# A two-block model on one core: the order of a linear layer's products, its waits, and its fillers

## The reference

```
first block:  proj = rmsnorm(x) @ w_in            (1024 x 3080), forgetting attention and chunked attention
              x += rmsnorm(y @ w_out)
              memory attention: h @ w_mq, mem @ w_mk, mem @ w_mv, o @ w_mo ; x += rmsnorm(...)
              x += rmsnorm(square(relu(h @ w_ff1)) @ w_ff2)
second block: mod = silu(c) @ ada_w + ada_b        (2 x 1024 x 6144)
              layer 0: gated 31-tap convolution (conv_in, depthwise conv, layer norm, silu, conv_out)
              layer 1: hgrn2 mixer (hgrn_in, a scan over time in both directions, hgrn_out)
              each followed by x += g2 * (square(relu(h @ w1)) @ w2)
out = rmsnorm(x)
```

## Time and profile before

| | |
|---|---|
| median of 3 runs | 2157.0 us |
| the profiled execution | 2156.95 us, its span 2155.2 us |
| TensorE (PE) busy | 2095.5 us, 97%, 10728 matmuls |
| VectorE (DVE) busy | 1237.6 us, 57% |
| ScalarE (ACT) busy | 826.2 us, 38% |
| GpSimd (POOL) busy | 202.1 us, 9% |
| mean granted TensorE clock | 0.995 of full speed |
| the chain that ended last | PE 84%, DVE 6%, ACT 5%, DMA 3% |
| linear layers' high products, line 1292 | 1672 and 768, 397 and 390 ns |

### The profile page before, as it was taken

The page is one execution under the profiler, slowest core; times in us unless marked ns, Lnnn a source line. Parts: engine busy times, 40 slices in busy tenths (PEclk is TensorE's granted clock), DMA queues, the critical chain, the costliest instruction groups (busy, mean ns, idle before and its releaser), DMA issues.

```text
span 2155.2 us, 26708 instructions
## 1 busy us (share of the span) xinstructions
PE 2095.5 (97%) x10728; PEld 1649.1 (77%) x10728; DVE 1237.6 (57%) x1895; ACT 826.2 (38%) x1326; POOL 202.1 (9%) x174
## 2 busy tenths in 40 slices
PE   8999999999999999999999999999999999999998
PEld 7777887678878876665788888787777777888886
DVE  5665745445677777887544344365675755443443
ACT  5345544445323233225423223344464454232231
POOL 1321011011000004453000000100000010000001
PEclk9999999999999999999999999999999999999999
DMA  6322422015677762662242332221121232323331
GB/s 202 98 66 90 137 97 92 25 59 206 223 270 249 259 230 87 164 168 82 81 133 97 97 99 89 62 69 50 59 69 50 69 105 83 106 98 98 98 98 40
DMA packets 218555, 245.51 MB, mean 114 GB/s; under 512 B 9144, under 2 KB 203192, under 8 KB 212288
## 3 DMA queue, kind: packets, MB, share of 16 engines
q1 hardware_dynamic: 208784, 231.71, 32.9%
q10 hardware_dynamic: 9648, 12.08, 2.2%
HBM read 237.73 MB, written 3.78 MB: 112 GB/s over the span
## 4 chain that ended last, share of the span: by engine, by line
PE 84%; DVE 6%; ACT 5%; DMA 3%; issue 2%; ACTq 1%; POOL 0%; SPq 0%; DVEq 0%; POOLq 0%
PE bank L1292 23%; PE bank L1293 23%; PE bank L1294 23%; PE bank L1313 2%; PE bank L1314 2%; PE bank L1315 2%; PE bank L1488 1%; PE bank L1359 1%; DVE wL L1881 1%; PE bank L1465 1%; PE bank L1372 1%; PE bank L1352 1%; DVE aacc L2078 1%; PE bank L1414 1%; ACT wH L1524 1%
## 5 line engine op out<-in xcount | busy, mean ns | idle before, releaser
L1292 PE MATMUL bank<-hH,wH 128*128 128x512 f32 (+1 forms) x1672 | 663.6, 397 | 22.0 <-DVE wL L1887 8.5
L1293 PE MATMUL bank<-hL,wH 128*128 128x512 f32 (+1 forms) x1672 | 645.9, 386 | 0.0
L1294 PE MATMUL bank<-hH,wL 128*128 128x512 f32 (+1 forms) x1672 | 645.9, 386 | 0.0
L1524 ACT ACTIVATE wH<-raw 128x1024 fp32r<-128x1024 f32 (+1 forms) x376 | 333.5, 937 | 371.9 <-PE bank L1294 292.8
L1881 DVE TENSOR_TENSOR wL<-raw,wH 128x1024 fp32r<-128x1024 f32 (+1 forms) x340 | 374.7, 1139 | 140.5 <-ACT wH L1524 140.5
L1292 PEld LDWEIGHTS bank<-hH,wH 128*128 128x128 f32 x1672 | 314.8, 188 | 114.4 <-issue 37.5
L1294 PEld LDWEIGHTS bank<-hH,wL 128*128 128x128 f32 x1672 | 314.9, 188 | 64.5
L1293 PEld LDWEIGHTS bank<-hL,wH 128*128 128x128 f32 x1672 | 315.3, 189 | 63.7 <-issue 4.1
L1292 PE MATMUL bank<-hidH,wH 128*128 128x512 f32 x768 | 299.9, 390 | 3.3 <-DVE hidL L2058 3.3
L1293 PE MATMUL bank<-hidL,wH 128*128 128x512 f32 x768 | 299.4, 390 | 0.0
L1294 PE MATMUL bank<-hidH,wL 128*128 128x512 f32 x768 | 299.4, 390 | 0.0
(11 more groups left out here) (217 smaller groups left out, 2049.9 us busy)
## 6 DMA issues: line engine op xcount, KB each, us to landing
raw<-in_mlp SPq DMA_DIRECT2D x64, 1024.0 KB, 5.4
araw<-in_ada_w SPq DMA_DIRECT2D x48, 1024.0 KB, 5.0
raw<-in_w_ff SPq DMA_DIRECT2D x32, 1024.0 KB, 7.3
raw<-in_hgrn_in SPq DMA_DIRECT2D x32, 512.0 KB, 3.7
raw<-in_w_in SPq DMA_DIRECT2D x11, 1024.0 KB, 5.3
raw<-in_conv_in SPq DMA_DIRECT2D x16, 512.0 KB, 4.1
u<-conv_u ACTq DMA_DIRECT2D x24, 270.0 KB, 5.0
raw<-in_w_mv SPq DMA_DIRECT2D x4, 1024.0 KB, 5.1
```

The lines of the kernel that those rows point to most:

```text
L1292: mm(out, wH[:, s, m:m + 128], xh[:, k, 0:width], start=k == 0, stop=False)
L1293: mm(out, wH[:, s, m:m + 128], xl[:, k, 0:width], start=False, stop=False)
L1294: i = mm(out, wL[:, s, m:m + 128], xh[:, k, 0:width], start=False, stop=k == KB - 1)
L1524: do(wH[:, s, c], raw[:, r, c], ACT.Copy).then_inc(*s_whi.up(n, x))
```

## The change

In the two branches of the tensor program that emit linear layers, a block's products are emitted in three passes over the tiles: wH hH for all tiles, wL hH for all, wH hL for all. Each pass is preceded by the waits for its own operand, so hL is waited for before the third pass. A weight half is waited for at the first block that reads it (`quarter`). Where there is one tile the order within a block changes from wH hH, wH hL, wL hH to wH hH, wL hH, wH hL. BUSY is 3 and not 4. Before hgrn_out, one owed weight low half is made, then activations 0 and 1 are split, then the other owed halves are made, and activation 2 is split after the layer's generator has been built (which emits nothing by itself).

```diff
-BUSY = 4
+BUSY = 3
...
         last_h = len(self.pieces) - 1
+        self.lows(1)
+        split(0)
+        split(1)
         self.lows()
         out = self.linear("hgrn_out", "hgrn_out", 0, 0, 1024, ("h", "ho"), self.to_x("r1x", (1, 2), "m1x", True), fresh=4,
                           step=1)
-        for j in range(3):
-            split(j)
+        split(2)
         next(last)
...
+        def quarter(n, k):
+
+            return k // 2 if n == 0 else k // 4
...
                         pe.wait_ge(*s_hi.at(*src[1:], k))
+                        for p in it["parts"]:
+                            pe.wait_ge(*s_whi.at(p["n"], quarter(p["n"], k)))
+                            out, s, m = banks[p["b"]][:, 0:width], p["n"] % NSPLIT, nc_ * k + p["m"]
+                            mm(out, wH[:, s, m:m + 128], xh[:, k, 0:width], start=k == 0, stop=False)
+                        for p in it["parts"]:
+                            pe.wait_ge(*low(p["n"]).at(p["n"], quarter(p["n"], k)))
+                            out, s, m = banks[p["b"]][:, 0:width], p["n"] % NSPLIT, nc_ * k + p["m"]
+                            mm(out, wL[:, s, m:m + 128], xh[:, k, 0:width], start=False, stop=False)
                         pe.wait_ge(*s_lo.at(*src[1:], k))
                         for p in it["parts"]:
-                            x = k // 2 if p["n"] == 0 else 1
-                            pe.wait_ge(*s_whi.at(p["n"], x))
-                            pe.wait_ge(*low(p["n"]).at(p["n"], x))
                             out, s, m = banks[p["b"]][:, 0:width], p["n"] % NSPLIT, nc_ * k + p["m"]
-                            mm(out, wH[:, s, m:m + 128], xh[:, k, 0:width], start=k == 0, stop=False)
-                            mm(out, wH[:, s, m:m + 128], xl[:, k, 0:width], start=False, stop=False)
-                            i = mm(out, wL[:, s, m:m + 128], xh[:, k, 0:width], start=False, stop=k == KB - 1)
+                            i = mm(out, wH[:, s, m:m + 128], xl[:, k, 0:width], start=False, stop=k == KB - 1)
                             if k == KB - 1:
                                 i.then_inc(*s_mm.up(*p["key"]))
```

More of the change, by code:

```diff
@@ L1301, in tensor_program @@
                     wl = wL[:, n % NSPLIT, :].rearrange("p (b n) -> p b n", b=KB)
-                    pe.wait_ge(*s_whi.at(n, 1))
-                    pe.wait_ge(*low(n).at(n, 1))
                     for k in it["ks"]:
@@ L1309, in tensor_program @@
                         pe.wait_ge(*s_hi.at(*src[1:], k))
+                        pe.wait_ge(*s_whi.at(n, quarter(n, k)))
+                        for p in it["parts"]:
+                            out, x = banks[p["b"]][:, 0:256], slice(128 * p["i"], 128 * p["i"] + 128)
+                            mm(out, xh[:, k, x], wh[:, k, :], start=k == 0, stop=False)
+                        pe.wait_ge(*low(n).at(n, quarter(n, k)))
+                        for p in it["parts"]:
+                            out, x = banks[p["b"]][:, 0:256], slice(128 * p["i"], 128 * p["i"] + 128)
+                            mm(out, xh[:, k, x], wl[:, k, :], start=False, stop=False)
                         pe.wait_ge(*s_lo.at(*src[1:], k))
@@ L1312, in tensor_program @@
                             out, x = banks[p["b"]][:, 0:256], slice(128 * p["i"], 128 * p["i"] + 128)
-                            mm(out, xh[:, k, x], wh[:, k, :], start=k == 0, stop=False)
-                            mm(out, xh[:, k, x], wl[:, k, :], start=False, stop=False)
                             i = mm(out, xl[:, k, x], wh[:, k, :], start=False, stop=k == KB - 1)
```

## The result

The changed kernel takes 2145.1 us (median of four runs, 2144.2 to 2146.9); the kernel before, run beside it on the same chip, 2158.0 (2156.5 to 2160.2). The ratio is 0.9935, 95% interval 0.9921 to 0.9949: 11.0 to 17.0 us faster, and 12.85 between the medians. The forecast was 2145.9. The profiled execution took 2144.15, its span is 2142.4, so the traces compare as 2155.2 against 2142.4. The code has grown, and lines of before L1292 / L1293 / L1294 are now L1295 (wH with hH), L1303 (wH with hL) and L1299 (wL with hH); most later lines moved by 13.

What follows compares the result with a forecast made beforehand. TensorE, busy 2095.5 of 2155.2 us, was taken as the bound, with only its waits at seams to win. 7.0 + 0.8 + 0.86 + 2.3 = 11.0 us off 2156.95 gave 2145.9, range 2142.0 to 2151.0.

Steps and rivals of the forecast that it cites:

- Part 1: Starts of linear layers: hL waited for behind two passes, so products start at hH's end; 7.0 us gained.
- Part 2: Weight halves, hgrn scan: second half waited for at block 4, not 0; 0.8 us gained, added waits free.
- part 4: New order before hgrn_out: hL made after one weight low half, so the scan's last sum starts earlier; 2.3 us gained.
- Part 3: Three fillers, not four: 0.86 us gained before the attention's output layer, elsewhere 0; clock effect counted as even, 0.
- the edge: At conv_out, idle time of 2.46 us with three fillers, close to where the clock might fall, at a price of 1.7.
- the 1.2 that I had named as the sign: Before hgrn_out, TensorE's 3.37 us of standing still should fall under 1.2.
- the wait for wL of 1.3: Before hgrn_out, a new second wait of about 1.3 us on the second piece's first weight low half.
- Given back behind the seam: Rival: VectorE bounds next in conv, ada part and scan; half of the 11.0 stays, 2151.5 us; chance 0.17.
- The slow clock goes too: Rival: shorter idle in the feed-forward and before hgrn_out keeps the clock up, 2 x 1.7 more, 2142.5 us; chance 0.11.
- The clock falls at the seams: Rival: one filler less makes the clock fall at eight further stages, 8 x 1.7 = 13.6 lost, 2159.6 us; chance 0.04.
- Added waits: Rival: 376 added waits hold up TensorE's weight loads; at 0.075 us each they cost 28 us, 2174; chance 0.04.
- Another operand ends where hL did: Rival: at the seams the change does not do what it says, 2156 us; chance 0.04.

Runs made afterwards that it cites:

- e5: Kernel before with a block's products in three passes only; hL still waited for with hH, whole weight pieces, four fillers, old order: 2159.13 us, ratio 0.9999.
- e1: Changed kernel, but hL waited for together with hH, ahead of the first pass: 2155.65 us, ratio 0.9984.
- e9: Kernel before with three passes and hL waited for ahead of the third; whole weight pieces, four fillers, old order: 2146.06 us, ratio 0.9947.
- e4: Changed kernel, but both halves of a weight piece waited for at its first block (first piece apart): 2145.96 us, ratio 0.9937.
- e2: Changed kernel with four fillers again instead of three: 2144.20 us, ratio 0.9932.
- e3: Changed kernel with the old order before hgrn_out (all owed weight low halves, then activations 0 to 2): 2145.45 us, ratio 0.9936.
- e11: Changed kernel itself, run once more for comparison: 2143.74 us, ratio 0.9933.
- e6: Changed kernel with one more, already met wait before each of 7320 linear-layer products: 2144.77 us, ratio 0.9941.
- e10: Changed kernel with fillers set by place, plus products on constants in three waits (attention values, memory attention, conv taps): 2140.88 us, ratio 0.9913.

## Why the prediction was right, point by point

The forecast of 2145.9 against 2145.1 is nearer than its working deserves. Part 1 carries it, and rightly. Part 2 and part 4, 3.1 us of the sum, priced edits that gave nothing beside the late hL. That the sum is met all the same is luck: the late hL by itself gave as much at hgrn_out as I had counted for the order, and falls of the clock that went and came nearly cancel.

**Part 1 (7.0 us) was right in mechanism and place, and a little small.** Where a seam stands by itself, the gain is as counted: 0.63 at the first product (0.8), 0.87 at the feed-forward's first layer (0.79), 0.67 at hgrn_in (0.78), 0.88 at the last MLP (0.78), 0.83 in the stretch from the last product of the conv's norm to conv_out's first (0.73). At the feed-forward hidL was expected to be waited for again after two products; row 607.61 shows it, third product 0.2 to 0.3 us late, and the stage gave about 1.0 instead of 0.8 once the clock is set apart: e5, with hidL first and no fall of the clock, takes 314.28 there, the changed kernel 313.31. The rest of the stage's 3.02 goes with the fall of the clock behind 608 that is not in this trace. The seams together are some 8 us; e1 and e9 show it from both sides.

**Part 2 (0.8) failed as a step, with its direction right.** The wL waits did vanish and the scan's first seven heads gained 0.60. But e4 has no wL waits in the scan either, without waiting by halves (its seven heads take 263.61, those of the other kernels with the late hL 262.97 to 263.96, but for e9 with a fall of the clock there, so 0.60 is within their spread). I had priced the halves against the old order of products, in which wL is the third product; with the passes it is behind a whole pass anyway. The added waits cost nothing that shows, as counted.

**Part 3 (0.86 and clock 0) was right at its place and is not there in the sum.** w_out's first product stands 2.18 us behind the start of the fillers instead of 3.03. The fillers of before start at 281.67, its first product is the first row below; the other two are the changed kernel's (I had put that start at 284.24 with three fillers; 0.86 ahead of this row is 283.84, and the gain is the same):

```profile
284.70 0.80 PE L1292 MATMUL bank<-hH,wH 128*128 128x512 f32 x1
```

```profile
283.30 2.74 PE L1353 MATMUL bank<-nacc,cst 128*128 128x512 f32 x6
285.48 1.03 PE L1295 MATMUL bank<-hH,wH 128*128 128x512 f32 x2
```

The price in this trace was the one I called the edge: idle 2.38 at conv_out for the predicted 2.46, and the clock at 0.61 in the window behind it, which costs 1.6 (94.91 against 93.30 in e2). I had counted the clock as even over the kernel. In these two traces it nearly was, by luck: it fell behind the wait ahead of the squares and in the conv in both, besides that before at 610 and 1736, and after at 196 and 985. Before, the fall in the conv lasted twice as long. There is no edge at this length: in the kernel before itself 2.35 us of idle time ahead of the squares (837.89) had a fall behind it (0.69 from 838 to 840), and the same 2.35 at conv_out had none. The prediction read the Trainium skill's advice against long idle gaps (TensorE: Matmul & The Clock Gate, "Why this matters for your kernels") as covering this seam. The gap that the page warns of is longer than 2.38 us, and in these runs the length alone does not decide: 2.38 and 2.66 us were followed by a fall, 2.70 and 3.26 us in e5 (at 608.91 and 1735.52) were not:

```profile
608.91 0.47 PE L1294 MATMUL bank<-hidH,wH 128*128 128x512 f32 x1 [2.70 <-DVE hidL L2071]
...
1735.52 1.16 PE L1294 MATMUL bank<-hH,wH 128*128 128x512 f32 x4 [3.26 <-DVE hL L2275]
```

```profile
608.00:612.00 4.00, 3.09 (x14) 2.61 (x15) 3.93 (x4) 1.93 (x3) 0.00 (x0) 1.00 1.07 375
...
1734.00:1738.00 4.00, 2.48 (x11) 2.08 (x12) 3.96 (x8) 2.10 (x5) 0.00 (x0) 1.00 1.05 355
```

**Part 4 (2.3) gave its number for another reason.** The last head gained 2.54, and the sum that I set at 1748.4 (from 1731.85, the start of the eight small products ahead of the seam, that is 16.55 on) came 16.68 us behind them, against 18.84 before. But e3 shows that the late hL does this by itself. The wait at the layer's start fell from 3.37 to 1.54 us, and not below the 1.2 that I had named as the sign (it is 0.96 in e11, the same kernel). Two errors: the wait for wL of 1.3 that I expected did not come, since VectorE had only one half behind the two hL; and what bounds the blocks behind the seam is not head 6 on its way to ScalarE's copies, but, for 0.95 us, the bank that VectorE's gate product frees. Nor is all of it the wait's: e5, hL first in the old order, had the full clock there by luck and took 17.16. So 1.7 of the 2.2 can be read as the clock, and 0.5 as products that start earlier. That the order can act, where hL is waited for first, e1 suggests against e5 (it also waits by halves): first product 3.28 us behind the eight small ones, not 4.42. With hL waited for behind the passes there is nothing left for it that shows.

**The rivals.** "Given back behind the seam": not seen in the whole, since all of the gain by seams, some 8 us, is in the measured time, and only the attention, behind the first products, lost anything, 0.8 us by a wait that grew (see below). "The slow clock goes too": in the feed-forward and at hgrn_out it went as that rival says, and came elsewhere. "The clock falls at the seams": at one of them, conv_out, that had kept it. "Added waits": excluded by e6. "Another operand ends where hL did": excluded by the rows at the seams.

**What stays open.** The 1.8 us between 11.0 and 12.8. Up to 1.7 of them are the clock's: what was not granted ahead of the last norm's sums (one minus the granted clock, times the length) comes to 8.5 us before and 6.8 after. The difference lies in the conv. Before, TensorE waited for `u` until 891.89, and the clock was low behind it for longer than after (to be set beside 0.73 in the changed kernel's 884 to 888, 0.84 in the next 4 us and 1.00 from there):

```profile
888.00:892.00 4.00, 0.11 (x4) 0.14 (x8) 3.86 (x6) 0.85 (x2) 2.58 (x3) 0.74 0.78 216
892.00:896.00 4.00, 4.00 (x20) 0.99 (x23) 1.63 (x3) 0.36 (x1) 0.00 (x0) 0.50 0.77 218
```

From the start of its first taps to that of its last the conv took 102.8 us instead of 105.5. The other traces with the late hL have 99.7 to 104.2 there, those with hL first 101.9 to 106.0, by how long the taps wait for `u` from memory. I cannot say from these runs whether the earlier start of conv_in helps there, or only chance. And by the estimate over all executions (under e1) some 12 us are left at an equal clock, so about 1 us stays without a cause.

From the first product to w_out's sums 2.26 us were lost, and this is not all chance. The wait before the values of one attention pair is 1.8 to 2.0 us in the four kernels that wait for hL first, and 2.2 to 3.4 in seven of the eight with the late hL and no filler there (1.04 in e4). In the changed kernel it is 2.66, at 195.25, and the clock was 0.57 behind it. So the late hL may cost some 0.8 us at this place, and a fall of the clock where one follows; why the wait grows no run here shows. The rows of both places, after:

```profile
195.25 0.88 PE L1385 MATMUL bank<-PTb,vt 128*64 128x128 f32 x12 [2.66 <-ACT PTb L1612]
...
885.81 2.77 PE L1427 MATMUL bank<-u,wd 128*32 128x512 f32 x12 [3.13 <-DMA u<-conv_u]
```

## What to carry over

When a product of split operands is summed from parts, give each part its own wait, and issue first all products whose operands are ready first, over all tiles of a block. Each seam gets back the time of the engine that makes the late part, here 0.6 to 0.9 us a seam and some 8 us in all. The added waits and the later emptying of the banks cost nothing that shows here. Price the parts of a change together: an order, a finer wait and this one all aimed at the same stall, and the late hL took it. A filler left out gives its own length back only where the operands come before it ends. Elsewhere it is cover for the clock, and belongs where TensorE really stands. And where runs of one kernel differ by as much as the parts of a change, set the mean granted clock beside each time before giving a part its price.

## What the runs showed that I had not expected

- 7320 waits that are already met, one before each product, don't change the spacing of 0.2263 us.
- The granted clock fell after waits of 1.65 (nine traces of thirteen), 2.38 and 2.66 us and not after 2.70, 3.20 and 3.26; the same kernel had it fall at the conv's taps in one run and not in the other (e11, 884 to 892: 1.00). A fall cost 1.6 to 1.7 us where a stage could be compared with and without it.
- Most of the spread between executions of one kernel goes with the mean granted clock: 1.7 us for 0.001 of it, so at an equal clock e10 is no faster than the changed kernel.
- Products on a constant in three waits, 14 in all, bring, with the fillers set by place, 3 to 4 us in a kernel that is 97% busy: four falls of the clock ahead of the tail (e11) become one.
